# Blocks of a mixture of experts ordered by expert, with weight rows gathered by computed numbers

## The reference

```python
glog = t @ router_g + router_g_b            # 4 groups
gw, gsel = softmax(glog) at its argmax
elog = (t @ router_e + router_e_b)          # 4 experts in each group
top_p, top_i = top_k(softmax(elog[gsel]), 2)   # 2 of the 4 experts of that group
top_p = top_p / sum(top_p)
for e in range(16):
    he = silu(t @ exp_w1[e]) * (t @ exp_w3[e])      # [1024, 256]
    y = y + comb[:, e:e+1] * (he @ exp_w2[e])       # [1024, 1024]
```

## Time and profile before

| | us |
|---|---|
| median of 3 runs | 3288.23 |
| the profiled execution, its own time | 3298.12 |
| span of the profiled execution, first to last instruction | 3296.3 |
| PE busy | 2843.3 (86%) |
| DVE busy | 1683.7 (51%) |
| ACT busy | 1230.4 (37%) |
| POOL busy | 173.4 (5%) |
| of this, the mixture of experts | about 2812 to 3296 |

### The profile page before, as it was taken

The page is one execution under the profiler, slowest core; times in us unless marked ns, Lnnn a source line. Parts: engine busy times, 40 slices in busy tenths (PEclk is TensorE's granted clock), DMA queues, the critical chain, the costliest instruction groups (busy, mean ns, idle before and its releaser), DMA issues. The chain is left out here.

```text
span 3296.3 us, 36022 instructions
## 1 busy us (share of the span) xinstructions
PE 2843.3 (86%) x13812; PEld 2226.4 (68%) x13812; DVE 1683.7 (51%) x2721; ACT 1230.4 (37%) x1968; POOL 173.4 (5%) x241
## 2 busy tenths in 40 slices
PE   5999997987776989996996999999989899488883
PEld 1767885656665868884674779987756588266772
DVE  3565544657776350013563355642134473677875
ACT  2544212445555231123342241111314411267776
POOL 0000000110000000000001000000000030011112
PEclk8999998999998999996888899999989999799997
DMA  5233443533302123222112313332253151489996
GB/s 223 82 122 133 160 150 108 152 100 90 81 17 84 48 70 137 87 79 84 44 56 88 130 56 104 117 115 89 96 175 88 35 188 45 163 311 344 381 367 237
DMA packets 144254, 431.57 MB, mean 131 GB/s; under 512 B 20002, under 2 KB 44322, under 8 KB 142804
## 3 DMA queue, kind: packets, MB, share of 16 engines
q1 hardware_dynamic: 100292, 265.08, 24.3%
q0 software_dynamic: 26512, 93.80, 8.3%
q10 hardware_dynamic: 17280, 70.39, 5.9%
HBM read 322.74 MB, written 106.47 MB: 130 GB/s over the span
## 5 line engine op out<-in xcount | busy, mean ns | idle before, releaser
L1092 PE MATMUL acc<-act_hi,w_hi 128*128 128x512 f32 (+3 forms) x2512 | 724.0, 377 | 66.2 <-DVE act_lo L849 45.2
L1092 PE MATMUL acc<-act_lo,w_hi 128*128 128x512 f32 (+3 forms) x2512 | 703.2, 369 | 0.0
L1092 PE MATMUL acc<-act_hi,w_lo 128*128 128x512 f32 (+3 forms) x2512 | 701.8, 368 | 0.0
L1092 PEld LDWEIGHTS acc<-act_hi,w_hi 128*128 128x128 f32 x2512 | 450.2, 190 | 171.1 <-DVE w_lo L754 59.0
L754 DVE TENSOR_TENSOR w_lo<-w_stage,w_hi 128x1024 fp32r<-128x1024 f32 x126 | 154.3, 1225 | 745.1 <-ACT w_hi L575 745.1
L1092 PEld LDWEIGHTS acc<-act_hi,w_lo 128*128 128x128 f32 x2512 | 447.6, 190 | 76.9
L1092 PEld LDWEIGHTS acc<-act_lo,w_hi 128*128 128x128 f32 x2512 | 448.3, 190 | 75.4
L575 ACT ACTIVATE w_hi<-w_stage 128x1024 fp32r<-128x1024 f32 x126 | 133.1, 1057 | 863.2 <-PE acc L1092 829.7
L2782 DVE TENSOR_TENSOR expert_lo<-expert_stage,expert_hi 128x1024 fp32r<-128x1024 f32 x186 | 226.3, 1224 | 82.4 <-ACT expert_hi L2719 80.1
L2719 ACT ACTIVATE expert_hi<-expert_stage 128x1024 fp32r<-128x1024 f32 x186 | 196.1, 1057 | 98.1 <-DMA expert_stage<-in_exp_w 53.8
L1928 DVE TENSOR_REDUCE max<-scores 128x1 f32<-128x256 f32 (+6 forms) x256 | 117.2, 484 | 149.1 <-PE scores L2069 148.2
(11 more groups left out here) (405 smaller groups left out, 4142.4 us busy)
## 6 DMA issues: line engine op xcount, KB each, us to landing
expert_stage<-in_exp_w SPq DMA_DIRECT2D x186, 512.0 KB, 6.5
w_stage<-in_w_in SPq DMA_DIRECT2D x43, 512.0 KB, 4.2
rope<-out_stage ACTq DMA_DIRECT2D x26, 640.0 KB, 3.6
proj<-out_stage ACTq DMA_DIRECT2D x26, 640.0 KB, 5.2
slots_out<-residual POOLq DMA_DIRECT2D x31, 512.0 KB
w_stage<-in_ab_w_in SPq DMA_DIRECT2D x26, 512.0 KB, 4.7
w_stage<-in_gla_w_in SPq DMA_DIRECT2D x25, 512.0 KB, 4.9
residual<-in_adaln_w POOLq DMA_DIRECT2D x24, 512.0 KB, 3.8
```

Of the source, the lines that this page charges most:

```text
L1092: mmi = eng.matmul(a[:, t, 0:n], lhs[:, j.w % 2, kb:kb + P], rhs[:, c0 + k, off:off + n], start=first, stop=last)
```

## The change

The blocks are now ordered by expert: all blocks of expert 0, then those of expert 1, and so on; the blocks that nobody needs are at the end and carry expert 15. So a block has the expert of the one before it, or the next one. The weights of an expert lie in three tensors of 16 x 128 rows of 8 KB (two units side by side): `exp_w0` and `exp_w1` for the up projections, `exp_w2` for the down projection. DVE computes a number for each partition and block, `w_row` = 128 * expert + partition, and where the block keeps the expert it adds 2048, so that the number lies past the end of the tensor. POOL gathers by these numbers with `bounds_check=NE * P - 1, oob_is_err=False`: rows out of bounds are left out, and the old contents stay. The stage is now three pairs of units with fixed places, not a ring: unit i of every block stands in `stage[:, i, :]`.

```diff
-        NS, R = 5, 8
+        R, NPAIR = 8, 3
-        stage = sb("expert_stage", [P, NS, D])
-        rows_of += [stage[:, NS - 1, :]]
+        stage = sb("expert_stage", [P, 2 * NPAIR, D])
+        rows_of = [fgain[:], stage[:, 4, :], stage[:, 5, :]]
...
-            ahead[j] = [n for n in range(start + R, end + R) if n < NU]
+            ahead[j] = [n for n in range(start + R if j else 4, end + R) if n < NU]
...
         def _(eng):                                        # SP
-            for n, (j, i) in enumerate(units):
...
-                if n >= NS:
-                    eng.wait_ge(w_lo, n - NS + 1)
-                if j < NE:
-                    src = dram["exp_w"][j][:, D * i:D * i + D]
...
-                eng.dma_start(stage[:, n % NS, :], src).then_inc(w_in[n % NS], 16)
+            def first_unit(i):
+                eng.dma_start(stage[:, i, :], dram["exp_w"][i // 2][0:P, D * (i % 2):D * (i % 2) + D]).then_inc(w_first[i], 16)
...
         def _(eng):                                        # POOL
+            def weights_in(j, c):
+                if 1 <= j < NTILE:
+                    eng.wait_ge(w_lo, number[j - 1, 2 * c + 1] + 1)
+                    eng.indirect_dma_start(
+                        out=stage[:, 2 * c:2 * c + 2, :].rearrange("p i n -> p (i n)"), out_offset=None, in_=dram["exp_w"][c][:, :],
+                        in_offset=bass.IndirectOffsetOnAxis(ap=w_row[:, j:j + 1], axis=0),
+                        bounds_check=NE * P - 1, oob_is_err=False).then_inc(w_in[c], 16)
...
             slots_in(0)
+            eng.wait_ge(experts_ready, 1)
+            weights_in(1, 0)
             slots_in(1)
+            weights_in(1, 1)
             for j in range(NTILE + 2):
                 if j + 2 < NTILE:
                     slots_in(j + 2)
                 if j >= 2:
                     expert_out(j - 2)
+                if j == 0:
+                    weights_in(2, 0)
+                weights_in(j + 2, 1)
+                weights_in(j + 1, 2)
+                weights_in(j + 3, 0)
...
             def round_w(n):                                # ACT
-                eng.wait_ge(w_in[n % NS], 16 * (n // NS + 1))
+                j, i = units[n]
+                if j:
+                    eng.wait_ge(w_in[i // 2], 16 * j)
+                else:
+                    eng.wait_ge(w_first[i], 16)
...
-            for n in range(4, R):
-                round_w(n)
             slots_hi(0)
...
                                                            # DVE
-            chain(eng.tensor_scalar(tmp[:], pos, float(P), None, ALU.is_ge))
-            chain(eng.tensor_tensor(tmp[:], tmp[:], adj[:].unsqueeze(1).to_broadcast([P, NTT, NE]), ALU.mult))
-            chain(eng.tensor_tensor(tmp[:], pos, tmp[:], ALU.add))
-            chain(eng.tensor_tensor(slot[:], tmp[:], col(rc, ROUTE_AT, "tile_at").unsqueeze(1).to_broadcast([P, NTT, NE]), ALU.add))
+            chain(eng.tensor_tensor(slot[:], pos, adj[:].unsqueeze(1).to_broadcast([P, NTT, NE]), ALU.add))
...
+            chain(eng.tensor_tensor(incl[:], incl[:], col(rc, ROUTE_AT, "expert_end"), ALU.add))
+            chain(eng.tensor_tensor(tcmp, col(rc, ROUTE_AT, "tile_no").unsqueeze(2).to_broadcast([P, NTILE, NE]),
+                                    incl[:].unsqueeze(1).to_broadcast([P, NTILE, NE]), ALU.is_ge))
+            chain(eng.tensor_reduce(texp[:], tcmp, AX, ALU.add))
+            chain(eng.tensor_scalar(texp[:], texp[:], float(NE - 1), None, ALU.min))
+            chain(eng.tensor_tensor(kept[:, 1:NTILE], texp[:, 1:NTILE], texp[:, 0:NTILE - 1], ALU.is_equal))
+            chain(eng.tensor_scalar(kept[:, 1:NTILE], kept[:, 1:NTILE], float(NE * P), col(rc, ROUTE_AT, "token_lo"), ALU.mult, ALU.add))
+            eng.scalar_tensor_tensor(w_row[:, 1:NTILE], texp[:, 1:NTILE], float(P), kept[:, 1:NTILE],
+                                     ALU.mult, ALU.add).then_inc(experts_ready, 1)
             eng.wait_ge(inverse_done, 1)
...
-            chain(eng.tensor_tensor(tcmp, col(rc, ROUTE_AT, "tile_no")[0:1, :].unsqueeze(2).to_broadcast([1, NSPARE, NE]),
-                                    incl[0:1, :].unsqueeze(1).to_broadcast([1, NSPARE, NE]), ALU.is_ge))
-            chain(eng.tensor_reduce(tsum[:], tcmp, AX, ALU.add))
-            eng.tensor_scalar(texp[:], tsum[:], float(NE - 1), None, ALU.min).then_inc(experts_ready, 1)
-            for n in range(4, R):
-                split_w(n)
-
             slots_lo(0)
```

More of the change, by code:

```diff
@@ L126 @@
 CONST_WIDTHS = [("ident", P), ("ones", P), ("headones", P), ("rot", P), ("causal", P), ("anti", P), ("invcnt", 2 * META)]
-ROUTE_WIDTHS = [("before", P), ("tile_end", 7), ("tile_at", 16), ("spare_off", 16), ("tile_no", 15), ("bound", NTILE + 1), ("column", P),
+ROUTE_WIDTHS = [("before", P), ("tile_end", 7), ("tile_at", 16), ("expert_end", 16), ("tile_no", NTILE), ("bound", NTILE + 1), ("column", P),
                 ("token_hi", 2 * NTT), ("token_lo", 1), ("order", 4)]
@@ L2568, in moe_phase @@
         sb, ps, sem = phase(nc, ctx)
-        NS, R = 5, 8
+        R, NPAIR = 8, 3
         flat = E.X[:].rearrange("p k n -> p (k n)")
         NU_ROWS = 3
-        rows_of = [sb(f"token_rows{i}", [P, D])[:] for i in range(1)]
         xs = flat[:, 8 * D:10 * D].rearrange("p (t n) -> p t n", n=D)
@@ L2618, in moe_phase @@
         u_stored = [sem(f"token_rows_stored{i}") for i in range(NU_ROWS)]
-        w_in = [sem(f"expert_loaded{i}") for i in range(NS)]
+        w_first = [sem(f"first_expert_loaded{i}") for i in range(2 * NPAIR)]
+        w_in = [sem(f"gp_expert_loaded{c}") for c in range(NPAIR)]
         w_hi, w_lo, used = sem("expert_hi_ready"), sem("expert_lo_ready"), sem("expert_used")
@@ L2630, in moe_phase @@
         block = ctx.enter_context(nc.Block())
-        units, first_up, first_down = [], {}, {}
+        units, first_up, first_down, number = [], {}, {}, {}
         for j in range(NTILE + 1):
@@ L2640, in moe_phase @@
         NU = len(units)
+        number = {u: n for n, u in enumerate(units)}
         ahead = {}
@@ L2715, in round_w @@
             def round_w(n):
-                eng.wait_ge(w_in[n % NS], 16 * (n // NS + 1))
+                j, i = units[n]
[3 more added lines that the diff above has]
+                    eng.wait_ge(w_first[i], 16)
                 if n >= R:
                     eng.wait_ge(used, n - R + 1)
-                eng.activation(whi[:, n % R, :], stage[:, n % NS, :], ACT.Copy).then_inc(w_hi, 1)
+                eng.activation(whi[:, n % R, :], stage[:, i, :], ACT.Copy).then_inc(w_hi, 1)
             def slots_hi(j):
@@ L2781, in split_w @@
                 eng.wait_ge(w_hi, n + 1)
-                eng.tensor_tensor(wlo[:, n % R, :], stage[:, n % NS, :], whi[:, n % R, :].bitcast(F32),
+                eng.tensor_tensor(wlo[:, n % R, :], stage[:, units[n][1], :], whi[:, n % R, :].bitcast(F32),
                                   ALU.subtract).then_inc(w_lo, 1)
@@ L3235, in build @@
             gemm_phase(nc, E, wts, jobs, feed)
-        moe_phase(nc, E, dict(router_w=d["router_w"], route=d["route"], norm2_row=d["norm2_row"], final_row=d["final_row"], exp_w=d["exp_w"],
+        moe_phase(nc, E, dict(router_w=d["router_w"], route=d["route"], norm2_row=d["norm2_row"], final_row=d["final_row"], exp_w=[d[f"exp_w{c}"] for c in range(3)],
                               normed=UD, expert_out=SY, y=d["y"]))
@@ L3312, in layout @@
         norm2_row=f["norm2_g_2"].reshape(1, D), final_row=f["final_g_2"].reshape(1, D),
-        exp_w=np.concatenate([up.reshape(NE, P, 4 * D), down.reshape(NE, P, 2 * D)], 2),
+        exp_w0=up[:, :, 0:4].reshape(NE * P, 2 * D), exp_w1=up[:, :, 4:8].reshape(NE * P, 2 * D), exp_w2=down.reshape(NE * P, 2 * D),
     )
```

39 lines of the change are left out of this document (17 added, 22 removed).

## The result

The changed kernel takes 3315.44 us (median of 8 runs, 3312.26 to 3319.69) where the kernel before takes 3294.34 on the same chip (8 runs, 3287.44 to 3304.46): a ratio of 1.0065, 95% interval 1.0053 to 1.0078. It is slower by about 21 us, and 3275 had been forecast. Of the 41 us between forecast and result, 6 come from the base: the forecast was set on 3288.23, a median of 3 runs, and 8 runs give 3294.34. The other 35 are the change, forecast at -13.5. The spans of the two profiled executions are 3313.4 and 3296.3 us, a difference of 17.1, and that is what the traces have to explain.

The account below looks back on a forecast made before the run. Late weights were taken to bound the expert blocks, delaying ACT, then DVE, then PE. Kept blocks -17.2, loading blocks +8.7 and start -5.0 summed to -13.5 us from 3288.23: forecast 3275 us, range 3252 to 3302.

Parts of the forecast that it names:

- Blocks that load: 15 blocks with a new expert, gathered by POOL in pairs: 12.0 us each instead of 11.42, +8.7 us.
- POOL's list holds up nobody in principle: Loading blocks: POOL's waits stand in DVE's split order and work queued behind them has slack; no separate cost.
- 1.5 to 2.5 us late, much as ACT waits now: Loading blocks: weight units come this late because token rows, results and other pairs share the queue; 12.0 us a block.
- my bound from below, 10.7 us: Loading blocks: lowest period considered, the fastest shown of the kernel before; the upper bound was 14.0 us.
- Blocks that keep: 13 periods whose expert stays: 10.1 us each instead of 11.42, with less traffic, -17.2 us.
- I take nothing: Empty gathers in kept blocks: still inside ACT's 6 us of room, so no cost; block bounded at 9.6 and 11.0 us.
- the end: Blocks 29 and 30, behind the last counted period: load nothing in time to matter, unchanged, 0 us.
- Rival 2: Kept blocks gain little, 11.0 us each, from late-issued skipped gathers or engines overlapping poorly: 3286 us, chance 0.20.
- The start: Before block 0: first slots gather issues faster once four DVE splits move behind it, -5.0 us.
- rival 3: Loading blocks: POOL starved by DVE's runs of splits, PE idle, clock falling; 14.0 us each, 3305 us, chance 0.17.
- Rival 4: Weight gathers: out-of-bounds rows still cost their transfer, every block at 12.0 us; 3299 us, chance 0.06.
- Rival 1: Loading blocks: weights arrive in time, 11.0 us each, start at -6.3; 3258 us, chance 0.19.

Follow-up runs that it names:

- kernel 1: Changed kernel with the leaving out undone, so all 90 weight gathers of blocks 1 to 30 bring their megabyte: 3351.1 us, 1.0177 of the kernel before.
- Kernel 5: Changed kernel with all 30 blocks loading, pairs issued by SyncE as plain DMAs instead of GpSimd's gathers: 3304.4 us, 1.0034 of the kernel before.
- kernel 6: Changed kernel's block order and start, but SyncE loads single units into five buffers for every block: 3294.1 us, 1.0000 of the kernel before.
- kernel 9: Changed kernel with all 30 blocks loading, GpSimd issuing the pairs as plain DMAs from the gathers' places: 3326.3 us, 1.0099 of the kernel before.
- kernel 7: Sorted blocks, six buffers freed unit by unit, SyncE plain DMAs, kept blocks' loads skipped by a SyncE branch: 3258.0 us, 0.9891 of the kernel before.
- kernel 2: Changed kernel with all 90 weight gathers issued and awaited but empty; all blocks use block 0's weights: 3270.8 us, 0.9925 of the kernel before.
- kernel 3: Changed kernel without any weight gathers or waits for them; all blocks use block 0's weights: 3249.9 us, 0.9859 of the kernel before.
- Kernel 10: Kernel before with only the start changed: units 4 to 7 rounded and split behind the first slots: 3285.4 us, 0.9973 of the kernel before.

## Why the prediction was wrong

**Blocks that load: +8.7 forecast, +33.3 measured.** This is the step that failed. I took 12.0 us and they took 13.8: 14 x (13.8 - 11.42) = 33.3. (I had counted 15 such periods; the second pair of block 2 falls ahead of them.) The single terms were near. An issue of "on the mean 1.5" was 1.2, the 1.9 us beside a split was as read from the earlier trace rows, and for a lone landing of 1 MB, which I put at 6.2 us, the fastest seen is 5.5 and the median 7.8 where all of them load (kernel 1). What failed is the sentence that "POOL's list holds up nobody in principle". I had checked that its waits stand in the order of the splits. I had not added up what stands between two gathers when several become ready together. Another pair's gather, the slots' gather and the store, 0.6 to 1.9 us each, made a needed gather start about 3 us after its split, with 2 MB issued just ahead of it in the one queue (3050.31 to 3055.07). The landing was then 8.4 us after the issue and 11.3 after the split, against some 7 us until ACT was free for it (3059.65) and the 6 that I had counted. Kernels 1, 5, 6 and 9 show the parts: 10, 22 and 25 us for the pair, GpSimd's list with its queue, and the gather's form, when all 30 blocks load. I also counted units "1.5 to 2.5 us late, much as ACT waits now". But before, 73 short waits left PE's granted clock at 0.97 from 2908 to 3188 us; after, 30 longer ones, with PE idle for up to 5.2 us at a time, left 0.91. And my bound from below, 10.7 us as the fastest period of the kernel before, was a misreading: it was the fastest that I showed, and one of the 28 takes 10.27 (block 19 to 20). It had no part in the miss.

**Blocks that keep: -17.2 forecast, -8.7 measured.** 14 x (10.8 - 11.42) = -8.7. The 10.1 us for a block without a late weight was right: 9.96 without gathers, 10.1 in kernel 7. "I take nothing" for an empty gather was wrong by 0.8 us a block: kernels 2 and 3. It was bounded at 11.0, and the truth lay next to the bound. Part of this is no loss: just ahead of the copy of block 28 ACT waits 3.3 us for an empty gather, that period is 12.1 and the next only 5.2, but together they are 17.4, as in kernel 3 without gathers (10.0 and 7.4). So 2.2 us belong to the end, which I had at nothing and which shows -2.4 above. Rival 2 had this half, with the reason that it gave (skipped gathers issued late behind POOL's waits).

**The start: -5.0 forecast, better than that.** From the end of the `slot_token` cast to the first copy it was 2912.39 - 2868.79 = 43.6 us before and 36.0 after: 7.6 gained. The path to `slot_token` grew by about 0.3 (0.6 forecast). The first copy came only 4.8 us earlier because the router of that execution began 2.5 us later (2849.16 for 2846.64); DVE was 2.4 us later already at 2790, in the layers ahead of this stage. What made it so no run shows. Kernel 10 gives 8.8 us for the start alone. The first gather's issue after was 1.03 us (timeline of POOL):

```profile
2872.51 1.03 POOL L2675 DMA_INDIRECT residual<-normed_tokens,slot_token  x1 [148.58 <-DVE slot_token L2908]
```

**The rivals.** The outcome, 3315, is beyond rival 3's 3305. Its price (14.0 us a load block, PE idle, the clock falling) is what happened. Its cause only in part: no gather took longer than 2.06 us in the rounds of any run, so POOL was not starved by runs of splits. In the long period above it was its own list that held it up. Rival 4 is refuted by the 47.2 MB, and by the DMA share of 0.34 in kernel 2. Rival 1 is refuted with gathers, but kernel 7 has it with plain DMAs: 10.5 us a loading block.

**What stays open.** Why the long periods come every second one and not at each load. The bunching is seen (no DMA at all, then over 410 GB/s), and it may be that ACT and DVE catch up after a long period, so that three pairs become ready close together; but no run changes the rhythm alone. Kernel 5, with pairs but from SyncE, does not have it; kernel 9, with the plain DMAs on GpSimd's list, does.

## What to carry to other kernels

A transfer that is put on another engine's list is late by what stands ahead of it there too, not by its bytes alone; add up the issues and the queued megabytes between "buffer free" and "needed", and compare with the room, at the moment when several are ready at once. Leaving transfers out pays (36 us here), but an issuing engine that has nothing else to do can leave them out by a branch, with no gather, and unit by unit instead of in pairs (57 us better together). When PE's waits are merged from many short ones into few long ones, count the clock that it loses behind each long one.

## What was not expected of the hardware

- A gather issued by GpSimd took 0.94 to 1.03 us alone and at most 2.06 beside splits in the rounds, but 5.49 at the start of the kernel before, where four splits ran back to back for 4.61 us; with these moved it took 1.03. That once it ended 0.9 us behind the whole run. A run does not do that by itself: beside runs of three (3.50 us) in the rounds it took 1.93, and of two gathers of weights beside a run of four (4.62 us from 2893.22 in the changed kernel), the one begun 0.25 us ahead of it took 1.00, the one begun inside it 1.21. What the difference is stays open.
- GpSimd's plain DMA with a computed address took 0.528 to 0.538 us in all 79 issues from 2905 to 3240 us, splits or not. The Trainium skill, "SBUF — State Buffer", section "SBUF: two separate sides", holds that a DMA issued by GpSimd cannot have its descriptors written while DVE holds the port pair that they share; a DVE operation with two inputs in SBUF, as the splits are, holds it only against a GpSimd operation that reads SBUF. The gathers agree with a lock (1.93 us beside a split against 1.03 or less alone); by the plain DMAs' issue times nothing of it is seen, though their landings (median 6.8 us) could hide a delay.
- An empty gather, with all of its numbers out of bounds, costs the issue of a full one: 1.20 us on the mean against 1.19. Each row left out still leaves a packet: kernels 1 and 2 and the changed one all show 131293, and those under 512 B grow from 18562 in kernel 1 to 24322 in the changed kernel, by 5760 = 45 x 128.
- The semaphore of a transfer is full only with the report of its last DMA engine. For the gather of 3055.38, 11 of the 16 engines had reported by 3061.96 and the last at 3063.80.
- SyncE's branches, two for each of six units a block, show no cost in the periods: the last seven of the 28, where nothing loads, take 9.95 to 9.99 us each, and without any gathers or loads it is 9.96.
